# Prompt attention: turns issued one by one between matmuls, and GpSimd's splits of weights and values as single operations in the drawn-up order

## The reference

```python
def _sb_block(q, qpos, k, v, kpos):
    scale = HEAD_DIM ** -0.5
    z = jnp.einsum('bqhd,bkhd->bhqk', q, k, preferred_element_type=jnp.float32) * scale
    causal = kpos[None, :] < qpos[:, None]
    log_keep = jnp.where(causal, jax.nn.log_sigmoid(-z), 0.0)
    rev = lax.cumsum(log_keep, axis=log_keep.ndim - 1, reverse=True)
    after = jnp.concatenate([rev[..., 1:], jnp.zeros_like(rev[..., :1])], axis=-1)
    log_a = jnp.where(causal, jax.nn.log_sigmoid(z) + after, -jnp.inf)
    a = jnp.exp(log_a)
    o = jnp.einsum('bhqk,bkhd->bqhd', a, v.astype(jnp.float32))
    return o.astype(q.dtype)
```

## Time and profile before

| | us |
|---|---|
| median of 3 runs | 2830.48 (2828.51 to 2833.29) |
| the profiled execution | 2826.52 |
| span of that execution, first to last instruction | 2824.9 |
| prompt attention, first score to last product | 1448.3 to 2532.7 |

### The profile page before, as it was taken

How to read it: one execution, slowest core, us unless ns; L and a number is a source line. 1 busy time by engine, 2 the same in 40 slices (tenths; PEclk the granted TensorE clock), 3 DMA queues, 4 the chain that set the end, 5 groups by cost and what they waited for, 6 DMA issues and landing times. The chain is left out here.

```text
span 2824.9 us, 42046 instructions
## 1 busy us (share of the span) xinstructions
PE 2767.3 (98%) x14856; PEld 2420.5 (86%) x14856; DVE 1642.8 (58%) x2152; ACT 1316.6 (47%) x2733; POOL 1157.2 (41%) x1023
## 2 busy tenths in 40 slices
PE   7999999999999999999989999999999999989998
PEld 6999999999988888889978888888888888868886
DVE  5321232123244450102249999999999999998775
ACT  6000000000033341111148888888888888875443
POOL 3333333333220020002356877777777768651110
PEclk9999999999999999999999999999999999999999
DMA  5101110111064444424578676777777876767773
GB/s 159 39 25 37 38 38 22 38 38 38 9 210 134 126 155 151 173 102 153 166 216 267 197 244 198 236 215 216 221 223 208 251 203 208 220 187 210 231 225 105
DMA packets 280359, 433.33 MB, mean 153 GB/s; under 512 B 52578, under 2 KB 218594, under 8 KB 274180
## 3 DMA queue, kind: packets, MB, share of 16 engines
q1 hardware_dynamic: 269156, 391.41, 45.5%
q0 software_dynamic: 11040, 39.86, 4.8%
HBM read 307.40 MB, written 123.81 MB: 153 GB/s over the span
## 5 line engine op out<-in xcount | busy, mean ns | idle before, releaser
L1989 POOL TENSOR_TENSOR a_a<-a_a,a_prod 128x512 f32<-128x512 f32 (+3 forms) x640 | 661.9, 1052 | 272.0 <-DVE a_prod L1939 196.6
L1939 DVE TENSOR_TENSOR_SCAN a_prod<-a_keep,a_prod,a_restart 128x513 f32<-128x513 f32 x384 | 478.2, 1269 | 8.3 <-ACT a_keep L1883 7.5
L1882 ACT ACTIVATE a_a<-a_pz 128x512 f32<-128x512 f32 (+3 forms) x640 | 357.2, 559 | 70.9 <-PE a_pz L1807 46.6
L1949 DVE TENSOR_TENSOR a_atl<-a_pt,a_ath 128x512 fp32r<-128x512 f32 (+3 forms) x640 | 363.1, 599 | 32.3 <-ACT a_ath L1892 29.0
L1883 ACT ACTIVATE a_keep<-a_pz 128x512 f32<-128x512 f32 (+3 forms) x640 | 361.1, 565 | 0.0
L1892 ACT ACTIVATE a_ath<-a_pt 128x512 fp32r<-128x512 f32 (+3 forms) x640 | 332.8, 558 | 57.5 <-PE a_po L1821 34.1
L1832 PEld LDWEIGHTS a_pt<-a_ident,a_bits 128*128 128x128 f32 x2176 | 232.2, 141 | 51.7 <-DVE a_atl L1949 8.1
L279 POOL TENSOR_TENSOR w_wh<-w_raw,w_gain 128x1024 fp32r<-128x1024 f32 x22 | 42.6, 1936 | 534.6 <-PE v_pg L349 279.9
L1806 PE MATMUL a_pz<-a_kh,a_q 128*128 128x512 f32 (+3 forms) x640 | 247.6, 390 | 8.4 <-ACT a_keep L1883 5.8
L1819 PE MATMUL a_po<-a_ath,a_v 128*128 128x512 f32 (+3 forms) x640 | 250.1, 395 | 2.3 <-POOL a_v L2000 1.5
L1832 PE MATMUL a_pt<-a_ident,a_bits 128*128 128x128 f32 x2176 | 244.8, 242 | 7.1 <-DVE a_atl L1949 4.7
(11 more groups left out here) (234 smaller groups left out, 6151.5 us busy)
## 6 DMA issues: line engine op xcount, KB each, us to landing
a_x<-x_d SPq DMA_DIRECT2D x84, 896.0 KB, 6.7
a_x<-x_d SPq DMA_DIRECT2D x56, 832.0 KB, 6.0
a_kh<-kh_t SPq DMA_DIRECT2D x32, 512.0 KB, 7.1
a_kl<-kl_t SPq DMA_DIRECT2D x32, 512.0 KB, 9.1
w_raw<-in_a_w_in POOLq DMA_DIRECT2D x30, 512.0 KB, 4.9
x<-f_xn POOLq DMA_DIRECT2D x17, 512.0 KB, 6.4
g_y_in<-sz_t SPq DMA_DIRECT2D x17, 512.0 KB, 7.6
g_x<-x SPq DMA_DIRECT2D x17, 512.0 KB, 4.1
```

The source lines that it names most:

```text
L1882: act.activation(a[:, s, q, 0:w], pz[:, n % ZS, 0:w], ACT.Sigmoid, scale=SCALE)
L1939: dve.tensor_tensor_scan(prod[:, s, 0:w + 1][:, ::-1], keep[:, n % KS, 0:w + 1][:, ::-1], restart[:, 0:1].broadcast_to([P, w + 1]), prod[: ...
L1949: dve.tensor_tensor(atl[:, b % AS, c0:], pt[:, turn_slot(pr, hh, b), c0:], ath[:, b % AS, c0:].bitcast(F32), ALU.subtract).then_inc(at_spl ...
L1989: pool.tensor_tensor(part, part, prod[:, n % PS, after:after + w], ALU.mult).then_inc(weighted, 1)
```

## The change

On TensorE a `turn` item issues only the first of its transposes; the others wait in a queue, `turns_left`. After every matmul of a score, a product or a chunk `between()` issues one of them, with the same operands as before. What is left is issued ahead of the next turn item, at a `rest` item, and at the end. `t_ready` is raised by the block's last transpose, wherever it stands. The planner puts in a `rest` item where, in its time, the engine starts something later than the last transpose would be seen. It counts 0.0595 us for a turn instead of 0.068, and 0.21 us later sight for each turn behind a block's first.

On GpSimd each operation of a split and of a value split becomes an item of its own in the list, so that others can be placed between; the subtraction of the values becomes two, of half the key tiles each (`v_ready` counts two per head).

```diff
-TURN = 0.068
+TURN, TURN_APART = 0.0595, 0.21
...
             if what == "turn":
-                return TURN * w / P, 0.2
+                return TURN * w / P, 0.2 + TURN_APART * (w // P - 1)
...
+        if engine == "PE":
+            if what != "turn" and start > self.turn_seen:
+                line.append(("rest", 0, 0, 0))
+            elif what == "turn":
+                self.turn_seen = end + seen
...
+SPLIT_TIMES, FILL_TIMES = (1.21, 0.69, 1.24), (1.12, 1.2, 1.2)
...
-                        sp.wait_ge(v_ready[hh], pr + 1)
+                        sp.wait_ge(v_ready[hh], 2 * (pr + 1))
...
                 pe.matmul(o, lhs, kh2[hh][:, p0:p0 + w], start=True, stop=False)
+                between()
                 pe.matmul(o, lhs, kl2[hh][:, p0:p0 + w], start=False, stop=True).then_inc(z_ready, 1)
+                between()
...
-                for q in range(block_from(b) // P, QG):
-                    mm = pe.transpose(pt[:, turn_slot(pr, hh, b), q * P:(q + 1) * P].bitcast(F32R),
-                                      a_bits[:, unit_slot(hh, u), q, j * P:(j + 1) * P], ident_r[:, :])
-                mm.then_inc(t_ready, 1)
+                turns_left.extend((pr, hh, b, q) for q in range(block_from(b) // P, QG))
+                turn_one()
+
+            def turn_one():
+                pr, hh, b, q = turns_left.popleft()
+                u, j = BLOCKS[b]
+                mm = pe.transpose(pt[:, turn_slot(pr, hh, b), q * P:(q + 1) * P].bitcast(F32R),
+                                  a_bits[:, unit_slot(hh, u), q, j * P:(j + 1) * P], ident_r[:, :])
+                if q == QG - 1:
+                    mm.then_inc(t_ready, 1)
+
+            def turn_rest():
+                while turns_left:
+                    turn_one()
+
+            def between():
+                if turns_left:
+                    turn_one()
...
                 elif what == "turn":
+                    turn_rest()
                     turn(pr, hh, n)
+                elif what == "rest":
+                    turn_rest()
...
-            def split_v(pr, hh):
+            def split_v(pr, hh, i):
...
+                else:
+                    tiles = slice((i - 1) * QT // 2, i * QT // 2)
+                    pool.wait_ge(v_hi[hh], pr + 1)
+                    pool.tensor_tensor(v2[hh][:, tiles, 1, :], v_in[:, hh, tiles, :], v2[hh][:, tiles, 0, :].bitcast(F32),
+                                       ALU.subtract).then_inc(v_ready[hh], 1)
```

More of the change, by code:

```diff
@@ L1293, in __init__ @@
         self.gates = [c for c in self.chunks if c[3] == PARTS - 1]
-        self.splits = [(un, m, half) for un in range(N_UN) for m in (Q, Z) for half in range(2) if (un, m) != (0, Q)]
-        self.splits.sort(key=lambda s: (s[0], s[1]))
+        self.splits = [(un, m, i) for un in range(N_UN) for m in (Q, Z) for i in range(2 * len(SPLIT_TIMES))
+                       if (un, m) != (0, Q)]
+        self.fills = [(h, i) for h in range(N_HEAD) for i in range(len(FILL_TIMES))]
         self.next = collections.Counter()
@@ L1299, in __init__ @@
                           for _, b in self.blocks)
-        self.spent = 0.0
+        self.spent, self.turn_seen = 0.0, 0.0
         for part in range(PARTS):
@@ L1395, in heads @@
                 yield "weigh", self.when(("scan", i["weigh"])), RANK["weigh"]
-            if i["values"] < N_HEAD:
-                h = i["values"]
+            if i["values"] < len(self.fills):
+                h, _ = self.fills[i["values"]]
                 yield "values", self.when(("v_in", h), self.back("product", (h + 1) * N_BLOCK - 1, 2 * N_BLOCK)), RANK["values"]
             if i["split"] < len(self.splits):
-                pr, m, half = self.splits[i["split"]]
+                pr, m, _ = self.splits[i["split"]]
                 yield "split", self.when(("raw", pr, m), ("used", pr - 1, m) if pr else ("used", None)), RANK["split"]
@@ L1432, in work @@
         if what == "values":
-            return 1.12 + 2.4, 0.1
+            return FILL_TIMES[self.fills[k][1]], 0.1
         if what == "split":
-            return 1.21 + 0.69 + 1.24, 0.1
+            return SPLIT_TIMES[self.splits[k][2] % len(SPLIT_TIMES)], 0.1
         w = PGROUPS[(self.chunks[k] if what == "chunk" else self.gates[k])[1]][1]
@@ L1490, in place @@
         elif what == "values":
-            line.append((what, *divmod(k, 2), 0))
-            at[what, k] = end
+            h, i = self.fills[k]
+            line.append((what, *divmod(h, 2), i))
+            if i == len(FILL_TIMES) - 1:
+                at[what, h] = end
             return
         elif what == "split":
[L1495 to L1498, removed]
+            pr, m, i = self.splits[k]
+            line.append((what, pr, m, i))
+            half, op = divmod(i, len(SPLIT_TIMES))
+            if op == len(SPLIT_TIMES) - 1:
+                at[what, pr, m, half] = end
+            if i == 2 * len(SPLIT_TIMES) - 1 and m == Z and pr + 1 < N_UN:
                 more = [("raw", pr + 1, m) for m in (Q, Z)]
@@ L1790, in _ @@
             pe.sem_inc(av_done, N_BLOCK)
+            turns_left = collections.deque()
             def score(pr, hh, n):
@@ L1815, in multiply @@
                 if b == 0:
-                    pe.wait_ge(v_ready[hh], pr + 1)
+                    pe.wait_ge(v_ready[hh], 2 * (pr + 1))
                 pe.wait_ge(at_split, blk(pr, hh, b) + 1)
@@ L1850, in chunk @@
                     pe.matmul(pq[:, 0:n], wh[m][:, kt, :], x_h, start=(kt == 0), stop=False)
+                    between()
                     pe.matmul(pq[:, 0:n], wh[m][:, kt, :], x_l, start=False, stop=False)
+                    between()
                     mm = pe.matmul(pq[:, 0:n], wl[m][:, kt, :], x_h, start=False, stop=(kt == KT - 1))
+                    if k < PART_KT - 1:
+                        between()
                 if part == PARTS - 1:
@@ L1989, in score, with split_gate @@
                 pool.tensor_tensor(part, part, prod[:, n % PS, after:after + w], ALU.mult).then_inc(weighted, 1)
-            def split_v(pr, hh):
-                pool.wait_ge(v_loaded[hh], 16 * (pr + 1))
-                if not is_pair(pr, 0):
-                    apart(pool, passed)
[L1996 to L2003, removed]
+            def split_v(pr, hh, i):
+                if i == 0:
+                    pool.wait_ge(v_loaded[hh], 16 * (pr + 1))
+                    if not is_pair(pr, 0):
+                        apart(pool, passed)
+                        pool.wait_ge(av_done, blk(pr, hh, 0))
+                    apart(pool, passed)
+                    pool.tensor_copy(v2[hh][:, :, 0, :], v_in[:, hh, :, :]).then_inc(v_hi[hh], 1)
+                else:
[3 more added lines that the diff above has]
+                                       ALU.subtract).then_inc(v_ready[hh], 1)
+            def split_gate(pr, m, i):
+                half, op = divmod(i, len(SPLIT_TIMES))
                 kts = slice(half * HK, (half + 1) * HK)
@@ L2008, in split_gate @@
                 w, w_h, w_l = raw[:, m, kts, :], wh[m][:, kts, :], wl[m][:, kts, :]
-                if half == 0:
-                    wait_past(pool, pq_ready[m], NGX * pr)
-                    wait_past(pool, raw_loaded[m], 16 * pr)
-                    apart(pool, passed)
[L2013 to L2018, removed]
+                if op == 0:
+                    if half == 0:
+                        wait_past(pool, pq_ready[m], NGX * pr)
+                        wait_past(pool, raw_loaded[m], 16 * pr)
+                        apart(pool, passed)
+                    pool.tensor_tensor(w, w, gain_b, ALU.mult).then_inc(w_scaled[m], 1)
+                elif op == 1:
+                    pool.wait_ge(w_scaled[m], 2 * pr + half + 1)
+                    apart(pool, passed)
+                    pool.tensor_copy(w_h, w).then_inc(w_hi[m], 1)
+                else:
+                    pool.wait_ge(w_hi[m], 2 * pr + half + 1)
+                    pool.tensor_tensor(w_l, w, w_h.bitcast(F32), ALU.subtract).then_inc(w_ready[m], 1)
             def do(what, pr, hh, n):
@@ L2023, in do @@
                 elif what == "values":
-                    split_v(pr, hh)
+                    split_v(pr, hh, n)
                 elif what == "split":
```

## The result

The changed kernel takes 2862.85 us (median of 4 runs, 2861.97 to 2864.97), the kernel before beside it 2830.94: a ratio of 1.0117, interval 1.0102 to 1.0132, or 32 us more. The forecast was 2851.5, with 2844 to 2860 as the case's own range and 2836 to 2870 as the wide one. Direction and mechanism held; the size was 21 where 32 came, outside the first range and inside the second.

What follows compares the result with a forecast made beforehand. TensorE's own order of work was taken to bound prompt attention. Profiled 2826.5 us + 21 for added runs, other terms 0, gave 2847.5; the median's 4.0 above made 2851.5, own range 2844 to 2860, wide range 2836 to 2870.

Steps and rivals of the forecast that it cites:

- TensorE's sequence sets the time: In prompt attention, 1490 to 2495 us, TensorE is nearly always busy, so what an instruction costs it is paid.
- A run costs 85n + 28 ns, from the exposed load: On TensorE, n turns in a row cost 85n + 28 ns; 834 more such runs cost +21 us.
- 1343 runs: TensorE's order under the new rule: 1343 runs instead of 464, 879 more, 45 of them free behind 128-column matmuls.
- The new order, taken as 0: Redrawn order in attention: delayed turns and shorter planned turns put at 0, ends -6 and +19 us.
- the later sight: A block's last turn lands 0.6 to 0.7 us later in attention; most of that delay meets slack.
- GpSimd's pieces: Split weight and value operations on GpSimd: 16 more instructions, 2.7 us there; ends -3.6 and +2.7, taken as 0.
- the shorter planned turn: Planner counts 59.5 ns a turn instead of 68, 18.5 us less in plan; others get more time, put at 0.
- 1 (the load hides): TensorE fetches the next weights under the long matmul ahead; a single turn costs 0.059 us, time 2785, chance 0.07.
- 2 (no effect): A turn's load takes an ordinary load's 0.11 us, or runs stay whole: no difference, 2830.5 us, chance 0.03.
- 3 (stalls won back): New order and short GpSimd pieces save up to 6 + 3.6 us, 2842, or 2827 with start and tail; chance 0.11.
- 4: Late turns stall TensorE in attention: +8 to +19 us on top of 21, 2860 to 2870; chance 0.17.
- the +19 allowed for late turns: Upper end for turns seen later: every tenth of the 640 blocks holds TensorE 0.3 us.

Runs made afterwards that it cites:

- experiment 1: The changed kernel's lists on every engine, but each block's turns issued whole where its item stands: 2836.5 us, ratio 1.0022 to the kernel before.
- experiment 2: The changed kernel's lists, but turns issued two at a time: 2848.2 us, ratio 1.0063 to the kernel before.
- experiment 5: Changed kernel with turns issued whole and the planned turn back at 0.068 us, later sight kept at 0.21: 2830.1 us, ratio 1.0001 to the kernel before.
- experiment 3: Kernel before with only GpSimd's splits as single operations, turns whole and planner's numbers as before: 2831.7 us, ratio 1.0003.
- experiment 6: Changed kernel with turns issued whole and no later sight, planned turn kept at 0.0595 us: 2837.4 us, ratio 1.0025 to the kernel before.

## Why the prediction was right, and what it mis-sized

*TensorE's sequence sets the time.* Right. The other engines' busy shares fell, while TensorE stayed busy and did less in the same time.

*A run costs 85n + 28 ns, from the exposed load.* Right as a mechanism: the load rows show it in the changed kernel, the line through 478, 842 and 1413 runs measures 27.8 ns a run, and taking runs away gave 6.9 us back. The size: I took 25 between 24 (by the loads) and 28 (by the fit). The fit, made of whole runs, was the better row. The loads' 108 less 84 leaves out what happens when the load after the ordinary one is a turn's again: the two starts are 0.13 us apart (1651.36, 1651.49), 132 ns in the middle of 1071 such places, where ordinary loads stand 0.11 apart. Part of it comes back, since over 512 columns the load behind then follows after 213 ns instead of 231 to 233; together that is 349 ns from turn to turn, where the loads alone give 339 (231 + 108). The kernel before has the same spacing, 134 ns, in 58 places behind matmuls of 256 or fewer columns.

*1343 runs.* 1413 came, since the order was drawn anew, and 27.8 is the mean of all added runs, those behind narrow matmuls among them. 834 x 25 = 21 should have been 935 x 27.8 = 26.0: 5 us of the 11 missed. The traces say the same by another way: over all of attention, the longer of stream and load, summed instruction by instruction, is 1040.4 us before and 1062.1 after, 21.7 more, and the intervals that lie less than 60 ns above it add 5.2.

*The new order, taken as 0.* This term failed; it is the other 6 us. Its parts separately: the later sight costs nothing, as I had argued from the slack (experiments 1, 2 and 5), and GpSimd's pieces at most 1 us (experiment 3). What I dismissed was the shorter planned turn: "a TensorE that is slower than its plan leaves the others more time". With 0.0595 and GpSimd's pieces the stretch grew from 1084 to 1092 (experiment 6). The largest part of the extra wait is the score's for the slot that ScalarE's sigmoids free. That a plan in which TensorE runs ahead of the truth puts scores too close is my reading of it and was not tested by itself. It can't be the whole rule either: 0.091 instead of 0.068 gained 4.5 us with whole turns, and 0.113, beside 0.068 with the same later sight, lost 5 us in the median and 8 in the stretch with spread ones. Each is one drawing-up, and what makes one order wait 11 us and another 27 stays open.

*Rivals.* 1 (the load hides) and 2 (no effect) are out by the load rows. 3 (stalls won back) didn't happen in the changed kernel; the orders with the later sight and the old number have 2 to 3 us less in gaps than before, too little to show. 4 named the right size, 8 to 19 us on top of 21, for a cause that did not act: late turns stalled nothing. The sign that the prediction gave for it, TensorE's waits at twice 13 us, came out between, at 21.2, and it took experiments 1 and 2 to decide. That the time lies inside the wide range is in part luck: it is owed to the +19 allowed for late turns, and what used it up were other waits.

*VectorE's share* was to fall to 0.94 and is 0.93 (966 of the 1040 us from 1490 to 2530). The stretch behind attention is unchanged, 292 us, and what lies ahead of it differs by no more than between two profiles of the kernel before.

## What to carry to other kernels

Price a small matmul by the start of the second instruction behind it, not of the next: the record shows a turn handing over after 0.06 us, and the engine has lost 0.11. In these traces a weight load hides only under the one matmul ahead (231 ns of a 512-column matmul cover a load of 108, 58 ns of a turn don't), so short matmuls with a load each belong together, best those with the shortest loads; breaking 478 runs into 1413 cost 26 us, gathering 464 into 239 gained 7. And in an order drawn up from planned durations, a changed constant gives a new order, which can cost or gain by itself (here up to 8 us): run the new order with the old instructions before judging either.

## What the runs showed of the hardware

By the starts of the loads, a turn's weight load takes 84 to 87 ns, an ordinary one of the same 128x128 size 108 to 110 (and the same in all twelve kernels). A turn's load directly behind an ordinary one that nothing hides starts 131 to 134 ns after it, also in all twelve. I know of no row that says why. And attention, some 17000 instructions on four engines (weight loads counted), repeated to 0.1 us in two profiles of the same kernel, while the phases ahead of it differed by 4.
